# One run for the high halves and one for the low halves in the stream's tile

## The chip, the cores and the metric

The kernel runs on one core of one Trainium2 chip. The metric is the device time of one execution in microseconds; the time before is 2694.59 us, the median of three runs (2694.45 to 2695.38).

## What is computed

One sequence of 256 tokens with 2048 features goes through two blocks. The first is a recurrent branch and a latent attention branch side by side, the second a differential attention layer, a stick-breaking attention layer and a convolutional feed-forward after each. Almost all arithmetic is products of a 256-token activation with a weight matrix of 2048 to 11264 columns:

```python
def second_block(x, positions, ...):
    h = x
    for layer in range(DEPTH_2):
        if layer < N_A_LAYERS:
            xn = _rmsnorm(h, attn_norm_g[layer])
            h = h + _diff_attention(xn, a_w_qkv[layer], ...)
        else:
            if layer == N_A_LAYERS:
                kv = _rmsnorm(h, kv_norm_g) @ b_w_kv
                ...
            xn = _rmsnorm(h, attn_norm_g[layer])
            h = h + _stick_breaking(xn, b_w_q[j], k_shared, v_shared, b_w_o[j])
        h = h + _conv_ffn(_rmsnorm(h, ffn_norm_g[layer]), ffn_w_up[layer], ...)
    return h
```

All tensors are float32, and the kernel has to come near float32 accuracy.

## The kernel before

**Products in halves.** The large products run in the one-pass format fp32r. A weight tile and an activation tile are each split into a high half (the value rounded to fp32r, written by ScalarE) and a low half (the rest, written by VectorE), both float32 words in SBUF. A product is then high x high, high x low and low x high. Line 703 issues two matmuls for each k-tile of 128 features and each block of 128 output rows: a **wide** one, whose moving operand has 512 columns (both halves of one side, against the high half of the other), and a **short** one with 256 columns (the high half of one side against the low half of the other). Their sums stand in the two halves of a PSUM bank and are added on the way out (L1805). In the last k-tile of a product the short one goes first.

**Who moves and who stands.** `unit_product` has two roles. In the usual one the weights (tile `wr`) are loaded into the array and the activation moves; the trace writes this as `acc<-stream,wr` or `acc<-ys,wr`. With `tokens_out` (the value heads of both attention layers) the activation is loaded and the weights move: `acc<-wr,stream`.

**The tiles.** `stream` holds the normalised activation of a layer, 16 k-tiles; in a k-tile its 256 high words are followed by its 256 low words (L363 to L367, `moving_tiles`). `ys` holds the input of an output projection or of a down projection in the same layout. Both begin 80 bytes past a multiple of 256 (`TILES_STEP` 64 and `MOVING_SHIFT` 16). `wr` is a ring of four units of four k-tiles each; its high halves form one run and its low halves another, 8400 bytes further on (`HALF_PAIR`, 2100 words): they begin 16 and 224 bytes past a multiple of 256. A wide matmul of the usual role so reads one run of 512 words, and one of the swapped role reads two runs of 256 words. The k-tiles and the 128-column blocks of all these tiles lie at multiples of 512 bytes from the tile's start, so each operand of a kind has the same place modulo 256 always.

**Order.** Each engine's program is written out by hand and runs in that order; semaphores tie them. SyncE loads `raw` from HBM (L485), ScalarE writes high halves of weights (L1327), VectorE low halves (L1795), TensorE multiplies (L703), VectorE reduces the accumulators (L1805). The activations' halves are written by ScalarE at L1333 (`split`) and by VectorE at L1828 (`lo`): for `stream`, 40 instructions each, two k-tiles at a time. TensorE's loads of the stationary operand (the LDWEIGHTS of each matmul, engine PEld) run beside the matmul ahead of them.

Of the kernel before, what the change touches and what calls it, by code (L numbers as in the profile page):

```python
# [25 lines left out]
P = 128  # L26
# [30 lines left out]
UK = 4  # L57
# [213 lines left out]
WEIGHTS_STEP, TILES_STEP, MOVING_SHIFT = 0, 64, 16  # L271
HALF_PAIR = 2 * UK * 256 + 52
# [32 lines left out]
def program(nc, t, out, consts):  # L305

    ctx = ExitStack()
    with ctx:
# [61 lines left out]
        ys = moving_tiles(nc.alloc_sbuf_tensor_at("ys", [P, GROUP * 2 * TOK + 2 * MOVING_SHIFT // 4], F32R, offset=base), GROUP)  # L370
# [297 lines left out]
        def _(pe):  # L668
# [397 lines left out]
            def woven_product(meanwhile):  # L1066

                T.lo_out.n += KT // 2
                ready, right = T.lo_out.n, lambda k: ys[:, k, :]
# [19 lines left out]
            def residual_product(blocks=KT, stored=False, tiles=2, gates=None, meanwhile=None):  # L1089
# [23 lines left out]
                def two_pairs(first):  # L1113
                    for e in range(2):
# [5 lines left out]
                        pair(lambda k: ys[:, k, :], blocks, before=gated if first and e == 0 else None, after=after)  # L1120
# [45 lines left out]
            def two_heads(first):  # L1166
                for e in range(2):
# [22 lines left out]
                    pair(lambda k: xs[:, k, :], before=None if live else normed, after=in_q)  # L1190
                    pair(lambda k: xs[:, k, :], before=lambda k: diff_sums(0) if k == UK + 1 else None, after=in_k)
                    pair(lambda k: xs[:, k, :], after=in_v, tokens_out=True)
# [18 lines left out]
            def ffn(last):  # L1211
# [8 lines left out]
                for g in range(2):  # L1220
                    if g == 0:
                        pair(lambda k: xs[:, k, :], before=normed_by, after=lambda n: stream_sums() if n == 1 else None)
                        pair(lambda k: xs[:, k, :])
                    with T.turns(pe, GROUP // 2 - (g == 0), **splits(2 * UK), acc_read=2):
                        for e in range(2):
                            pair(lambda k: xs[:, k, :])
# [12 lines left out]
            pair(lambda k: xs[:, k, :], before=normed_by, after=lambda n: stream_sums() if n == 1 else None)  # L1239
            pair(lambda k: xs[:, k, :])  # L1240
            for part in range(2):
                if part == 1:
                    tokens_roots(1 + 3 * A_HEADS + 2)
                with T.turns(pe, B_HEADS // 4 - 1, **splits(8), acc_read=2):
                    for e in range(2):
                        pair(lambda k: xs[:, k, :], tokens_out=part == 1)
            for e in range(2):
                pair(lambda k: xs[:, k, :], tokens_out=True)
# [28 lines left out]
            def two_query_pairs(first):  # L1277

                for e in range(2):
# [11 lines left out]
                    pair(lambda k: xs[:, k, :], before=normed if first and e == 0 else at_tile, after=after)  # L1291
# [19 lines left out]
        def _(act):  # L1311
# [33 lines left out]
            def norm_splits(n):  # L1345

                for _ in range(n):
                    g = norms[0] % (KT // 2)
                    norms[0] += 1
                    split((xs[:, 2 * g:2 * g + 2, 0:TOK], tmp[g % 2][:, :, :]))  # L1350
# [143 lines left out]
            def att_split(it):  # L1494
                act.wait_ge(F.mixed_read.sem, 4 + it)
                f(ys[:, 8 + 2 * it:10 + 2 * it, 0:TOK], tmp[0][:, :, :], ACT.Copy).then_inc(T.hi_out.sem, 1)

            def rnn_split(it):
                split((ys[:, 2 * it:2 * it + 2, 0:TOK], S[1][:, :, :]))
# [51 lines left out]
            def residual_product(units=8, squares=True, stored=False, ahead=0, table=True, woven=False):  # L1551
# [7 lines left out]
                def two_pairs(first, i=None):  # L1559
                    for e in range(2):  # L1560
                        hi(2 if first and woven else units // 2 - (ahead if first and e == 0 else 0))
                        if squares:
# [3 lines left out]
                            split((xs[:, tiles, 0:TOK], tmp[e][:, :, :]))  # L1566
# [44 lines left out]
            def diff_out_split(tiles):  # L1611
                split((ys[:, tiles, 0:TOK], tmp[0][:, :, :]))
# [58 lines left out]
            def ffn(last):  # L1671
                def pair_of_tiles(tile, e, rooted=False):
# [7 lines left out]
                    split((ys[:, tile, 0:TOK], tmp[e][:, 0:1, :]))  # L1680
# [52 lines left out]
            def stick_split(tiles):  # L1733
                split((ys[:, tiles, 0:TOK], tmp[0][:, :, :]))
# [39 lines left out]
        def _(dve):  # L1774
# [50 lines left out]
            def lo(to, src):  # L1825

                dve.wait_ge(*T.hi_out.next())
                tt(to[:, :, TOK:2 * TOK], src, to[:, :, 0:TOK], ALU.subtract).then_inc(*T.lo_out.one())  # L1828

            def norm(value, splits=()):  # L1830

                for g in range(KT // 2 + 1):
# [6 lines left out]
                    if g:  # L1839
                        if g == KT // 2:  # L1840
                            own(T.split_me)
                        lo(xs[:, 2 * g - 2:2 * g, :], tmp[(g - 1) % 2][:, :, :])
# [338 lines left out]
            def att_lo(it):  # L2181
                lo(ys[:, 8 + 2 * it:10 + 2 * it, :], tmp[0][:, :, :])
# [13 lines left out]
            def rnn_lo(i):  # L2196
                own(T.split_me)
                lo(ys[:, 2 * i:2 * i + 2, :], S[1][:, :, :])
# [37 lines left out]
            def residual_product(blocks=KT, gain=None, stored=False, gated=False, first_splits=4, woven=False):  # L2236
# [3 lines left out]
                def two_pairs(first, i=None, final=False):  # L2240
                    for e in range(2):
# [18 lines left out]
                        if gain is not None:  # L2260
# [10 lines left out]
                            lo(xs[:, tiles, :], tmp[e][:, :, :])  # L2271
# [60 lines left out]
            def diff_out_lo(tiles):  # L2332
                own(T.split_me)
                lo(ys[:, tiles, :], tmp[0][:, :, :])
# [52 lines left out]
            def ffn(layer):  # L2387
# [4 lines left out]
                def pair_of_tiles(g, ds, e):  # L2392
# [14 lines left out]
                    lo(ys[:, ds(0), :], tmp[e][:, 0:1, :])  # L2407
# [81 lines left out]
            def stick_lo(tiles):  # L2489
                lo(ys[:, tiles, :], tmp[0][:, :, :])  # L2490
# [73 lines left out]
```

## Time and profile before

| | |
|---|---|
| median of three runs | 2694.59 us |
| the profiled execution | 2694.55 us |
| its span, first to last instruction | 2692.5 us |
| TensorE busy | 2679.0 us, 99% of the span |
| TensorE weight loads | 2345.8 us, 87% |
| VectorE busy | 1978.9 us, 73% |
| ScalarE busy | 1198.1 us, 44% |
| DMA | 64% of the 16 engines' time, 196 GB/s |
| granted clock of TensorE | 1.00 in all slices (2.4 GHz) |

The profile is of one execution. A line of the costliest groups gives the source line, the engine, the operation, the tiles written and read, the size, the count, then busy time and mean duration in ns, then the idle time just before these instructions. The duration of a matmul is from its first column to its last result, and the next one begins long before that: what a matmul costs TensorE is the distance from its start to the next start, and this has to be read from how many of them run in a stretch.

### The profile page before, as it was taken

How to read it: one execution, taken by the hardware profiler on the slowest of the kernel's cores; microseconds unless marked ns; L12 is line 12 of the kernel's file. 1: busy time of each engine (PE TensorE's matmuls, PEld its weight loads, DVE VectorE, ACT ScalarE, POOL GpSimd, SP SyncE). 2: the span in 40 equal slices, each digit the busy share in tenths (PEclk: the TensorE clock that was granted, in tenths of full speed). 3: DMA queues.
4: the chain of work that ended last, by engine and by line, in shares of the span. 5: the costliest groups of instructions: out<-in, count | busy, mean ns of one | idle time of the engine just before them, and what ended most of it. 6: DMA issues, size and time to landing. Idle time of an engine off the chain costs nothing.

```text
span 2692.5 us, 44098 instructions
## 1 busy us (share of the span) xinstructions
PE 2679.0 (99%) x15292; PEld 2345.8 (87%) x15292; DVE 1978.9 (73%) x2594; ACT 1198.1 (44%) x1533; POOL 5.7 (0%) x12
## 2 busy tenths in 40 slices
PE   9999999999999999999999999999999999999999
PEld 7888888888888888888888888888888888888888
DVE  6647577777777788667887676698878876688865
ACT  2004355555554444444444443366444444444443
POOL 0000000000000000000000000000000000000000
PEclk9999999999999999999999999999999999999999
DMA  9986665555556666666666666644566666666664
GB/s 349 358 278 191 204 192 192 163 175 162 161 163 194 190 192 193 197 190 192 193 190 187 201 196 188 190 154 140 186 191 195 193 188 197 188 195 195 191 203 149
DMA packets 705762, 528.14 MB, mean 196 GB/s; under 512 B 32206, under 2 KB 694544, under 8 KB 705424
## 3 DMA queue, kind: packets, MB, share of 16 engines
q1 hardware_dynamic: 701728, 523.60, 63.8%
q10 hardware_dynamic: 3951, 3.44, 0.4%
q8 instruction: 52, 0.85, 0.1%
q14 instruction: 31, 0.25, 0.0%
HBM read 523.80 MB, written 2.10 MB: 195 GB/s over the span
## 4 chain that ended last, share of the span: by engine, by line
PE 96%; DVE 2%; DMA 1%; ACT 0%; issue 0%; SPq 0%; DVEq 0%; ACTq 0%
PE acc L703 81%; PE acc L819 3%; PE acc L1013 2%; PE acc L807 2%; PE turned L819 2%; PE sums L819 2%; PE mixed L934 1%; PE sums L1151 1%; DVE pro_ada L1869 1%; DVE wr L1795 0%; PE scores L1144 0%; PE sums L719 0%; PE mixed L935 0%; DMA pro_xrow<-in_x 0%; PE sums L890 0%; PE scores L920 0%
## 5 line engine op out<-in xcount | busy, mean ns | idle before, releaser
L703 PE MATMUL acc<-stream,wr 128*128 128x512 f32 (+1 forms) x7680 | 1328.5, 333 | 0.3 <-DVE wr L1795 0.3
L703 PEld LDWEIGHTS acc<-stream,wr 128*128 128x128 f32 x7680 | 1159.0, 188 | 156.1 <-issue 3.8
L1795 DVE TENSOR_TENSOR wr<-raw,wr 128x1024 fp32r<-128x1024 f32 x832 | 998.6, 1222 | 317.2 <-ACT wr L1327 307.7
L1327 ACT ACTIVATE wr<-raw 128x1024 fp32r<-128x1024 f32 x832 | 871.2, 1058 | 695.4 <-PE acc L703 682.5
L703 PE MATMUL acc<-ys,wr 128*128 128x512 f32 (+1 forms) x4352 | 747.4, 332 | 0.9 <-DVE wr L1795 0.9
L703 PEld LDWEIGHTS acc<-ys,wr 128*128 128x128 f32 x4352 | 655.7, 188 | 87.3 <-DVE wr L1795 1.5
L703 PE MATMUL acc<-wr,stream 128*128 128x512 f32 (+1 forms) x1024 | 182.7, 338 | 0.0
L703 PEld LDWEIGHTS acc<-wr,stream 128*128 128x128 f32 x1024 | 157.0, 188 | 22.5 <-issue 0.5
L1679 ACT ACTIVATE ffn_cv<-ffn_cv 128x256 f32<-128x256 f32 x88 | 36.9, 419 | 245.5 <-DVE ffn_cv L2401 245.5
L1805 DVE TENSOR_REDUCE ffn_ug<-acc 128x512 f32<-128x1024 f32 x88 | 107.8, 1225 | 35.2 <-PE acc L703 35.2
L1828 DVE TENSOR_TENSOR ys<-tmp,ys 128x256 f32 (+3 forms) x108 | 51.3, 475 | 76.0 <-ACT ys L1333 73.4
L1869 DVE SCALAR_TENSOR_TENSOR pro_ada<-aring,small,pro_ada 128x512 f32<-128x512 f32 (+1 forms) x103 | 85.7, 833 | 22.9 <-DMA aring<-in_w_ada 17.0
L1805 DVE TENSOR_REDUCE S<-acc 128x512 f32<-128x1024 f32 x72 | 87.9, 1221 | 19.7 <-PE acc L703 19.7
L1333 ACT ACTIVATE ys<-tmp 128x256 f32 (+3 forms) x104 | 46.8, 450 | 106.4 <-DVE tmp L2405 102.0
L1809 DVE TENSOR_TENSOR ffn_ug<-ffn_ug,rx 128x512 f32<-128x512 f32 x88 | 60.9, 692 | 3.0
L807 PE MATMUL acc<-xm,w 128*128 128x256 f32 x256 | 58.4, 381 | 0.7 <-DVE xm L1889 0.4
L1013 PE MATMUL acc<-xm,w 128*128 128x256 f32 x256 | 57.3, 379 | 0.0
L807 PEld LDWEIGHTS acc<-xm,w 128*128 128x128 f32 x256 | 48.2, 190 | 8.9 <-issue 1.9
L1013 PEld LDWEIGHTS acc<-xm,w 128*128 128x128 f32 x256 | 47.7, 190 | 6.0
L2399 DVE SCALAR_TENSOR_TENSOR ffn_cv<-ffn_ug,vcol,ffn_cv 128x256 f32<-128x256 f32 x88 | 42.7, 485 | 13.2 <-DVE ffn_cv L2396 13.0
L2401 DVE SCALAR_TENSOR_TENSOR ffn_cv<-ffn_ug,vcol,ffn_cv 128x256 f32<-128x256 f32 x88 | 42.7, 485 | 13.0 <-DVE ffn_cv L2399 12.8
L2396 DVE TENSOR_SCALAR ffn_cv<-ffn_ug,vcol 128x256 f32<-128x256 f32 x88 | 36.4, 413 | 16.5 <-DVE ffn_ug L1809 16.4
(324 smaller groups left out, 1482.9 us busy)
## 6 DMA issues: line engine op xcount, KB each, us to landing
raw<-in_ffn_w_up SPq DMA_DIRECT2D x704, 256.0 KB
raw<-in_ffn_w_down SPq DMA_DIRECT2D x160, 512.0 KB
raw<-in_a_w_qkv SPq DMA_DIRECT2D x96, 512.0 KB
raw<-in_b_w_kv SPq DMA_DIRECT2D x64, 512.0 KB
aring<-in_w_ada SPq DMA_DIRECT2D x96, 256.0 KB, 6.6
w<-in_w_in SPq DMA_DIRECT2D x48, 512.0 KB
raw<-in_w_ada SPq DMA_DIRECT2D x32, 512.0 KB, 4.9
raw<-in_w_out SPq DMA_DIRECT2D x32, 512.0 KB
```

The costliest lines, as they stand in the source:

```text
L703: mm = pe.matmul(*ops, start=first and ops is wide, stop=last and ops is wide)
L807: pe.matmul(bank(c // 2)[:, (c % 2) * TOK:(c % 2 + 1) * TOK], w[:, c * P:(c + 1) * P], xm[:, k, :], start=False, stop=k == KT - 1 and c % ...
L819: mm = pe.matmul(out(j), *here, start=k == 0, stop=k == UK - 1)
L1013: mm = pe.matmul(bank(b + j)[:, 0:TOK], w[:, k, j * P:(j + 1) * P], xm[:, u * UK + k, :], start=u == 0 and k == 0, stop=u == 3 and k == UK ...
L1327: f(half_of(0, s), raw[:, s, :], ACT.Copy)\
L1333: f(to[0], to[1], ACT.Copy).then_inc(T.hi_out.sem, 1)
L1795: tt(half_of(1, s), raw[:, s, :], half_of(0, s), ALU.subtract).then_inc(T.unit_split[s].sem, 1)
L1805: dve.tensor_reduce(out_tiles, a[:, 0:tiles, :].rearrange("p t (b c) -> p t c b", b=2), axis=AX_X, op=ALU.add)\
L1809: tt(out_tiles, out_tiles, both(rx), ALU.mult).then_inc(*T.acc_read.one())
L1828: tt(to[:, :, TOK:2 * TOK], src, to[:, :, 0:TOK], ALU.subtract).then_inc(*T.lo_out.one())
L1869: stt(here, aring[:, n % ADA_RING, 0:2 * kn * P], small[:, 8 + r:9 + r], here, ALU.mult, ALU.add)\
L2399: step(stt(cv[e][:, :], UG[e][:, 1, 1:1 + TOK], taps[1], cv[e][:, :], ALU.mult, ALU.add))
```

## The change

The tile `stream` gets another layout: the high halves of all 16 k-tiles stand in one run of 16384 bytes, the low halves in a second run that begins 128 bytes after the end of the first. High halves begin at the same 80 bytes modulo 256 as before; low halves began at 80 too and now begin at 208. The tile is 256 bytes longer, so what is allocated behind it keeps its place modulo 256. `ys` and `wr` stay as they are; `ys` is only indexed with one dimension more.

```diff
@@ -269,6 +269,7 @@
 WEIGHTS_STEP, TILES_STEP, MOVING_SHIFT = 0, 64, 16
+LOWS_SHIFT = 128
 HALF_PAIR = 2 * UK * 256 + 52
@@ -356,18 +357,18 @@
-        stream = sb("stream", [KT * 2 * TOK + 2 * MOVING_SHIFT // 4], F32R)
-        xs_at = nc.sbuf_base - KT * 2 * TOK * 4 - 2 * MOVING_SHIFT
-
-        def moving_tiles(tensor, tiles):
-
-            return tensor[:, MOVING_SHIFT // 4:MOVING_SHIFT // 4 + tiles * 2 * TOK].rearrange("p (k n) -> p k n", k=tiles)
-
-        xs = moving_tiles(stream, KT)
+        run = KT * TOK + LOWS_SHIFT // 4
+        stream = sb("stream", [2 * run + 2 * MOVING_SHIFT // 4], F32R)
+        xs_at = nc.sbuf_base - 2 * run * 4 - 2 * MOVING_SHIFT
+
+        xs = stream[:, MOVING_SHIFT // 4:MOVING_SHIFT // 4 + 2 * run].rearrange("p (h r) -> p h r", h=2)[:, :, 0:KT * TOK]\
+            .rearrange("p h (k n) -> p k h n", k=KT)
@@ -694,11 +695,11 @@
                         if tokens_out:
-                            wide = (a[:, j, :], x[:, cols], both_halves)
-                            short = (a[:, j, 0:256], x[:, 256 + j * P:256 + j * P + P], high)
+                            wide = (a[:, j, :], x[:, 0, cols], both_halves)
+                            short = (a[:, j, 0:256], x[:, 1, cols], high)
                         else:
                             wide = (a[:, j, :], high[:, cols], x)
-                            short = (a[:, j, 0:256], low[:, cols], x[:, 0:TOK])
+                            short = (a[:, j, 0:256], low[:, cols], x[:, 0, :])
@@ -1825,7 +1826,7 @@
-                tt(to[:, :, TOK:2 * TOK], src, to[:, :, 0:TOK], ALU.subtract).then_inc(*T.lo_out.one())
+                tt(to[:, :, 1, :], src, to[:, :, 0, :], ALU.subtract).then_inc(*T.lo_out.one())
```

The rest of the diff is the same change of index at each use of `xs` and `ys`. No instruction is moved, and each engine's program has the same operations in the same order and of the same sizes. Two things differ in form: the halves that ScalarE and VectorE write to `stream` are one run of 512 words (two k-tiles) instead of two runs of 256, and VectorE issues 8 register instructions fewer for their addresses.

## Rows read from the trace of the kernel before

**Rows 1.** The page: engines, share of the span, and TensorE's granted clock
```profile
PE 2679.0 (99%) x15292; PEld 2345.8 (87%) x15292; DVE 1978.9 (73%) x2594; ACT 1198.1 (44%) x1533; POOL 5.7 (0%) x12
...
PEclk9999999999999999999999999999999999999999
```

**Rows 2.** The page: the chain that ended last, by engine and line
```profile
PE 96%; DVE 2%; DMA 1%; ACT 0%; issue 0%; SPq 0%; DVEq 0%; ACTq 0%
PE acc L703 81%; PE acc L819 3%; PE acc L1013 2%; PE acc L807 2%; PE turned L819 2%; PE sums L819 2%; PE mixed L934 1%; PE sums L1151 1%; DVE pro_ada L1869 1%; DVE wr L1795 0%; PE scores L1144 0%; PE sums L719 0%; PE mixed L935 0%; DMA pro_xrow<-in_x 0%; PE sums L890 0%; PE scores L920 0%
```

**Rows 3.** TensorE's groups by shape over the whole span (count | busy us, mean ns)
```profile
L703 PE MATMUL acc<-stream,wr 128*128 128x512 f32 x3840 | 1314.9, 391 | 0.3 <-DVE wr L1795 0.3
L703 PE MATMUL acc<-stream,wr 128*128 128x256 f32 x3840 | 1037.9, 275 | 0.0
L703 PE MATMUL acc<-ys,wr 128*128 128x512 f32 x2176 | 741.6, 389 | 0.9 <-DVE wr L1795 0.9
L703 PE MATMUL acc<-ys,wr 128*128 128x256 f32 x2176 | 590.0, 275 | 0.0
L703 PE MATMUL acc<-wr,stream 128*128 128x512 f32 x512 | 180.6, 396 | 0.0
L703 PE MATMUL acc<-wr,stream 128*128 128x256 f32 x512 | 140.8, 280 | 0.0
```

**Rows 4.** Matmuls running in stretches of 85 us: usual role (stream), swapped role, usual role (ys)
```profile
1240.00:1325.00 85.00, 85.00 (x501) 1.00 0.68 194
1668.00:1753.00 85.00, 85.00 (x488) 1.00 0.62 186
1110.00:1195.00 85.00, 85.00 (x501) 1.00 0.63 195
```

**Rows 5.** Groups by shape in 1240 to 1325 us, usual role
```profile
L703 PE MATMUL acc<-stream,wr 128*128 128x512 f32 x251 | 85.0, 388 | 0.0
...
L703 PE MATMUL acc<-stream,wr 128*128 128x256 f32 x250 | 67.7, 275 | 0.0
```

**Rows 6.** Groups by shape in 1668 to 1753 us, swapped role
```profile
L703 PE MATMUL acc<-wr,stream 128*128 128x512 f32 x244 | 84.8, 394 | 0.0
...
L703 PE MATMUL acc<-wr,stream 128*128 128x256 f32 x244 | 67.2, 280 | 0.0
```

**Rows 7.** Plain float32 matmuls of 256 columns in 110 to 125 us
```profile
110.00:125.00 15.00, 15.00 (x71) 1.00 1.06 403
```

**Rows 8.** ScalarE's and VectorE's writes to stream and ys, by shape
```profile
L1333 ACT ACTIVATE stream<-tmp 128x512 f32 x24 | 15.2, 634 | 3.7 <-DVE tmp L2263 0.9
L1828 DVE TENSOR_TENSOR stream<-tmp,stream 128x512 f32 x24 | 16.6, 693 | 7.4 <-ACT stream L1333 7.4
L1809 DVE TENSOR_TENSOR S<-S,rx 128x512 f32<-128x512 f32 x16 | 11.1, 692 | 0.5
L1600 ACT ACTIVATE sq<-S 128x512 f32<-128x512 f32 x16 | 10.1, 632 | 16.1 <-DVE S L1809 16.1
```

**Rows 9.** All waits of TensorE: who it waited for, us, times, longest
```profile
PE turned L724 <- DMA cst<-in_constants: 4.9, 1, 4.9
PE turned L1110 <- DVE ffn_fin L2258: 2.0, 1, 2.0
PE acc L703 <- DVE wr L1795: 1.2, 3, 0.5
```

More of the change, by code:

```diff
@@ L1119, in after @@
                                 meanwhile(n)
-                        pair(lambda k: ys[:, k, :], blocks, before=gated if first and e == 0 else None, after=after)
+                        pair(lambda k: ys[:, k, :, :], blocks, before=gated if first and e == 0 else None, after=after)
                 per = dict(acc_read=2, **splits(2 * -(-blocks // UK)))
@@ L1188, in in_v @@
                             diff_out_sums()
-                    pair(lambda k: xs[:, k, :], before=None if live else normed, after=in_q)
-                    pair(lambda k: xs[:, k, :], before=lambda k: diff_sums(0) if k == UK + 1 else None, after=in_k)
-                    pair(lambda k: xs[:, k, :], after=in_v, tokens_out=True)
+                    pair(lambda k: xs[:, k, :, :], before=None if live else normed, after=in_q)
+                    pair(lambda k: xs[:, k, :, :], before=lambda k: diff_sums(0) if k == UK + 1 else None, after=in_k)
+                    pair(lambda k: xs[:, k, :, :], after=in_v, tokens_out=True)
             two_heads(True)
@@ L1221, in ffn @@
                     if g == 0:
-                        pair(lambda k: xs[:, k, :], before=normed_by, after=lambda n: stream_sums() if n == 1 else None)
-                        pair(lambda k: xs[:, k, :])
+                        pair(lambda k: xs[:, k, :, :], before=normed_by, after=lambda n: stream_sums() if n == 1 else None)
+                        pair(lambda k: xs[:, k, :, :])
                     with T.turns(pe, GROUP // 2 - (g == 0), **splits(2 * UK), acc_read=2):
                         for e in range(2):
-                            pair(lambda k: xs[:, k, :])
+                            pair(lambda k: xs[:, k, :, :])
                     residual_product(GROUP, stored=g == 1 and last, tiles=1)
@@ L1237, in normed_by @@
                     pe.wait_ge(T.lo_out.sem, ready + k // 2 + 1)
-            pair(lambda k: xs[:, k, :], before=normed_by, after=lambda n: stream_sums() if n == 1 else None)
-            pair(lambda k: xs[:, k, :])
+            pair(lambda k: xs[:, k, :, :], before=normed_by, after=lambda n: stream_sums() if n == 1 else None)
+            pair(lambda k: xs[:, k, :, :])
             for part in range(2):
@@ L1245, in _ @@
                     for e in range(2):
-                        pair(lambda k: xs[:, k, :], tokens_out=part == 1)
+                        pair(lambda k: xs[:, k, :, :], tokens_out=part == 1)
             for e in range(2):
-                pair(lambda k: xs[:, k, :], tokens_out=True)
+                pair(lambda k: xs[:, k, :, :], tokens_out=True)
             def stick_scores():
@@ L1290, in at_tile @@
                             stick_sums(0)
-                    pair(lambda k: xs[:, k, :], before=normed if first and e == 0 else at_tile, after=after)
+                    pair(lambda k: xs[:, k, :, :], before=normed if first and e == 0 else at_tile, after=after)
             two_query_pairs(True)
@@ L1611, in diff_out_split @@
             def diff_out_split(tiles):
-                split((ys[:, tiles, 0:TOK], tmp[0][:, :, :]))
+                split((ys[:, tiles, 0, :], tmp[0][:, :, :]))
             def two_heads(first, i=None):
@@ L1733, in stick_split @@
             def stick_split(tiles):
-                split((ys[:, tiles, 0:TOK], tmp[0][:, :, :]))
+                split((ys[:, tiles, 0, :], tmp[0][:, :, :]))
             def two_query_pairs(first, i=None):
@@ L2181, in att_lo @@
             def att_lo(it):
-                lo(ys[:, 8 + 2 * it:10 + 2 * it, :], tmp[0][:, :, :])
+                lo(ys[:, 8 + 2 * it:10 + 2 * it, :, :], tmp[0][:, :, :])
             def rnn_gate(i):
@@ L2197, in rnn_lo @@
                 own(T.split_me)
-                lo(ys[:, 2 * i:2 * i + 2, :], S[1][:, :, :])
+                lo(ys[:, 2 * i:2 * i + 2, :, :], S[1][:, :, :])
             F.scores_ready.n, F.scores_read.n = 8, 8
@@ L2333, in diff_out_lo @@
                 own(T.split_me)
-                lo(ys[:, tiles, :], tmp[0][:, :, :])
+                lo(ys[:, tiles, :, :], tmp[0][:, :, :])
             def two_heads(first, i=None):
@@ L2406, in pair_of_tiles @@
                     own(T.split_me)
-                    lo(ys[:, ds(0), :], tmp[e][:, 0:1, :])
+                    lo(ys[:, ds(0), :, :], tmp[e][:, 0:1, :])
                     split_units(3)
@@ L2489, in stick_lo @@
             def stick_lo(tiles):
-                lo(ys[:, tiles, :], tmp[0][:, :, :])
+                lo(ys[:, tiles, :, :], tmp[0][:, :, :])
             def two_query_pairs(first, i=None):
```

19 lines of the change are left out of this document (10 added, 9 removed).

## The prediction

> **What bounds the kernel now.** I read the engines' line first: TensorE is busy 2679.0 us of 2692.5, at a granted clock of full speed in every slice [rows 1]. That line alone would not do, since matmuls are recorded with their latency and overlap, so I looked at the chain that ended last, which is TensorE for 96% and line 703 for 81% [rows 2], and at TensorE's waits, the longest three of which add up to 8.1 us in the whole program [rows 9]. So nothing is gained by making another engine faster, and each nanosecond on a matmul of line 703 is a nanosecond of the kernel. What one costs is read from a stretch in which nothing else runs. In 85 us of the usual role 501 matmuls are running [rows 4], that is 250.5 pairs of a wide and a short one, or 339.3 ns a pair; `ys` gives the same count. In 85 us of the swapped role there are 488, or 244 pairs of 348.4 ns. (Each count takes in the one or two that run across the edge, in all three stretches alike; so the difference, 9.1 ns, is better than the level.) The whole program has 3840 pairs in the usual role on `stream`, 2176 on `ys` and 512 in the swapped role [rows 3].
>
> **What the change touches.** Four things, and no instruction count or order on TensorE, ScalarE, SyncE or GpSimd.
>
> First, the moving operand of 3840 wide matmuls is two runs of 256 words, the second 128 bytes further on modulo 256, instead of one run of 512. Usual pairs with two runs do not occur in the trace of before, so the price is bounded by the nearest rows. Wide matmuls with two runs exist in the swapped role, there with 208 bytes between the places: their mean is 394 ns against 388 for those with one run, 6 ns more [rows 5, 6]. But the short matmuls beside them, which read a single run in both roles, are slower by 280 - 275 = 5 ns as well [rows 5, 6]. So what the swapped role pays is paid by both kinds, and the part that only the jump between two runs can have caused is 6 - 5 = 1 ns at most, within the rounding of the rows. The whole-span rows say the same: 396 - 391 = 5 and 280 - 275 = 5, so 0 [rows 3]. The 5 ns that both pay I put down to how the loaded and the moving operand lie to each other, since this is what differs for both: in the usual role the moving words begin at 80 and the loaded ones at 16 or 224 modulo 256, in the swapped one the moving ones at 16 and the loaded ones at 80. The value I take for the jump is 0 ns. The ends are: up, 3840 x 9.1 ns = +35 us, if all of the swapped role's surplus comes from jumps; down, what the low half of a wide matmul could at best give back. For that the nearest row is the plain float32 matmuls, which pass 256 columns twice: 71 are running in 15 us, 211 ns each, or near 216 with the two at the edges left out, so 108 ns for a pass of 256 columns [rows 7]. A third of an fp32r pair is 339.3 / 3 = 113.1 ns. The low half of a wide one could so fall by 113 - 108 = 5 ns, 3840 x 5 = -19 us, and no run of 256 fp32r columns in the usual role is that fast in these rows.
>
> Second, in the swapped role the low half of the activation is the loaded operand of the 512 short matmuls, and its place goes from 80 to 208. It is loaded while the wide one before it runs, whose first run begins at 16. The distance of moving to loaded was 16 - 80 = 192 modulo 256; it becomes 16 - 208 = 64. In the usual role the high weights are loaded under a short matmul at 80 - 16 = 64, and those pay nothing. If 64 is good here too, the surplus of the wide matmul, about half of the 9.1 ns of the pair, goes: 512 x 4.5 = -2.3 us. The high half stays at 80, and the short ones keep their 5 ns. The ends are 0 and 512 x 9.1 = -4.7 us, or the same the other way, +2.3 us, if the new place is the worse.
>
> The Trainium skill (SBUF — State Buffer, section "A bandwidth-pool intuition that's wrong") gives TensorE a read port for the moving operand and a second, independent one for LDWEIGHTS. By that rule no place of one can matter for the other, this term would be 0, and the total below would be higher by its 2.3 us. The rows speak against it: the same short matmul with 256 columns takes 280 ns in one role and 275 in the other [rows 5, 6].
>
> Third, ScalarE's and VectorE's 40 writes each to `stream` become one run of 512 words. With two runs they take 634 and 693 ns; the same operations on one run of 512 take 632 and 692 [rows 8]. So 80 instructions gain 1 to 2 ns each, 0.1 us, and most lie beside matmuls. TensorE is not among those that wait for them in its three longest waits [rows 9]. 0 us.
>
> Fourth, 8 register instructions fewer on VectorE, which stands idle 27% of the span [rows 1]: 0 us. The waits do not change, since the same semaphores count the same instructions.
>
> The sum: 0 - 2.3 + 0 + 0 = -2.3 us. The profiled execution took 2694.55 us, 2.05 more than its span and 0.04 less than the median of the runs; so 2694.55 - 2.3 = 2692.3 us, and the same against the median. What a measurement here can tell from no change is about 0.2%, or 5.4 us: this is the same time.
>
> **The rivals.** *The jumps cost.* The swapped role is then slow because the place modulo 256 changes inside each wide matmul and again at the next short one, and reading has to fall into step again; the short ones' 5 ns are the step back. In the usual role everything moving began at 80 modulo 256 and nothing ever changed its place; after the change it goes 80, 208, 80 in every pair. For it: the two roles differ in this more than in anything else, and it explains both 5 ns at once. Against it: within the swapped role the step forward (208 bytes) and the step back (48) are unlike, and cost the same 5 ns. Its price is 3840 x 9.1 = +35 us, so 2692.3 + 35 = 2727 us; at half the price, with only the wide ones paying, +17 and 2710 us. It decides the sign from 1.4 ns a pair (5.4 us / 3840) on, with the 2.3 us of the swapped role kept.
>
> *The usual role gets faster.* An fp32r pair takes 339.3 ns where three passes at the pace of the float32 rows are 3 x 108 = 324 [rows 4, 7]. If what slows them is a clash between reads of the moving and of the loaded operand, a low half at another place than the high half can miss the clash. With the low half of the wide one relieved of 5 ns this gives 2692.3 - 19 = 2673 us. Against it: the load of 128 columns runs beside the first part of a wide matmul, and the low half is its second part; and stream and ys, in different places of SBUF and with different work beside them, both stand at 501 in 85 us [rows 4], which looks like a pace of the format rather than a clash. The Trainium skill (TensorE: Matmul & The Clock Gate, section "Back-to-back issue gap") has N/2.4 + 2.5 ns for one matmul. By it a wide and a short one would take 215.8 + 109.2 = 325 ns, an estimate from that page, and the kernel stands 14 ns a pair above it; nothing in it says that a layout could get there.
>
> *It does nothing at all,* also not in the swapped role: the ports are independent and both surpluses come from the format of the operands. Then 2694.6 us.
>
> **How the numbers follow.** The forecast (jump free, the swapped role gains some) has 0.44, with its own range of 2688 to 2698 from the ends of the second term and 1 ns on the first. Nothing at all has 0.05. The jumps cost their full price: 0.14. They cost between 1 and 5 ns a pair (+4 to +19 us): 0.13, nearly all of it over 0.2%. The usual role gets faster: 0.24, mostly between -6 and -26 us. Adding up by sign: faster by over 0.2% (under 2689.2 us) 0.24 and 0.02 of the forecast's lower edge, 0.26; slower by over 0.2% (over 2700.0) 0.14 + 0.12 = 0.26 and 0.01, so 0.27; the rest, 0.47, is the same. The likeliest is the forecast, 2692.3. The range goes from 2668 (a gain of 5 ns a wide matmul and a little on the short ones) to 2730 (the full price of the jumps and 3 us): outside are some 0.07 of larger gains and 0.05 of larger losses.
>
> **What would show it.** The count of matmuls in 85 us of a feed-forward stretch on `stream` is the test: 501 again for the forecast, 488 for jumps at full price, 505 or more where the usual role gets faster (85 us / 334 ns is 254 pairs, 508). The stretches on `ys` must stay at 501; should they move too, it is not the layout of `stream`. In the swapped role the count should go from 488 to 494 or so (85 us / 343.9 ns), with the wide ones' mean down from 394 towards 389 and the short ones at 280. ScalarE's L1333 and VectorE's L1828 should stand at 632 and 692 ns. The prediction is wrong from its first term if the wide matmuls' mean on `stream` leaves 388 ns by more than 1.

## The result and the profile after

The changed kernel takes 2725.77 us (median of five runs, 2725.38 to 2726.08), the kernel before 2694.79 us in the same comparison (2694.45 to 2695.38): a ratio of 1.0115, 95% interval 1.0104 to 1.0126. It is 31.0 us slower. The forecast of "the same" was wrong; the time is close to the one of the first rival, 2727 us, and inside the stated range (2668 to 2730) only because that rival's full price set its upper end.

The page of the changed kernel, engines and clock, to be laid beside [rows 1]:

```profile
PE 2711.6 (100%) x15292; PEld 2363.6 (87%) x15292; DVE 1981.3 (73%) x2594; ACT 1198.5 (44%) x1533; POOL 5.7 (0%) x12
...
PEclk9999999999999999999999999999999999999999
```

TensorE is busy 32.6 us longer with the same 15292 matmuls at the same granted clock, and the other engines do what they did. TensorE's groups by shape over the whole span, to be laid beside [rows 3]:

```profile
L704 PE MATMUL acc<-stream,wr 128*128 128x512 f32 x3840 | 1343.2, 395 | 0.1
L704 PE MATMUL acc<-stream,wr 128*128 128x256 f32 x3840 | 1054.8, 280 | 0.0
L704 PE MATMUL acc<-ys,wr 128*128 128x512 f32 x2176 | 741.9, 389 | 0.9 <-DVE wr L1796 0.9
L704 PE MATMUL acc<-ys,wr 128*128 128x256 f32 x2176 | 590.2, 275 | 0.0
L704 PE MATMUL acc<-wr,stream 128*128 128x512 f32 x512 | 182.2, 398 | 0.0
L704 PE MATMUL acc<-wr,stream 128*128 128x256 f32 x512 | 141.2, 281 | 0.0
```

Nearly all of the loss is on the stream in the usual role: the recorded durations of the wide matmuls go from 391 to 395 ns, and those of the short ones, whose moving words, loaded words and places have not changed at all, from 275 to 280. The `ys` groups stand where they stood. The matmuls running in 85 us show the price; the second stretch lies a little later than in [rows 4], since the swapped role now comes later (columns: stretch, its length, TensorE busy and matmuls running, clock, DMA share, GB/s):

```profile
1240.00:1325.00 85.00, 85.00 (x489) 1.00 0.64 182
1690.00:1775.00 85.00, 85.00 (x484) 1.00 0.61 185
1110.00:1195.00 85.00, 85.00 (x502) 1.00 0.62 194
```

On the stream 489 for 501: 2 x 85 us / 489 = 347.7 ns a pair, 8.3 ns more, x 3840 pairs = +32 us. In the swapped role 484 for 488: 351.2 ns a pair, 2.8 ns more, x 512 = +1.4 us, where a gain of 2.3 had been forecast. `ys` stands at 502 for 501. These sum to 33 us. TensorE is busy 32.6 us longer and idle 1.0 us less (12.5 us for 13.5), so the span grew by 2724.1 - 2692.5 = 31.6 us. Counts of whole matmuls are no better than 0.7 ns a pair. ScalarE's and VectorE's writes to the stream are unchanged, where the third term had them 1 to 2 ns shorter, without any consequence for the time [rows 8]:

```profile
L1829 DVE TENSOR_TENSOR stream<-tmp,stream 128x512 f32 x24 | 16.6, 693 | 5.1 <-ACT stream L1334 4.9
...
L1334 ACT ACTIVATE stream<-tmp 128x512 f32 x24 | 15.2, 634 | 3.1
```

So all of the time is in how close matmuls of the stream follow each other. In what follows a tile's price is its pair time less that of the kernel before, counted in two stretches that lie within the same stage in every kernel: 1245 to 1330 us for the stream and 1120 to 1205 us for `ys`. The kernel before has there

```profile
1245.00:1330.00 85.00, 85.00 (x501) 1.00 0.67 191
1120.00:1205.00 85.00, 85.00 (x502) 1.00 0.63 195
```

so 339.3 and 338.6 ns a pair, and the changed one

```profile
1245.00:1330.00 85.00, 85.00 (x489) 1.00 0.65 187
1120.00:1205.00 85.00, 85.00 (x502) 1.00 0.63 195
```

One matmul more or less is 0.7 ns a pair. "Place" is where a tile's words begin, modulo 256 bytes. The places of before: moving 80, high weights 16, low weights 224.

A count gives the price of a pair, and a recorded duration does not give that of one matmul. For this the trace's start times serve: the mean distance from the start of a matmul to the start of the next one, over all neighbouring pairs of the stream in the usual role (3671 or 3672 distances of either kind; those over 300 ns, where TensorE paused, are left out). The level comes out 1 ns higher than by the counts.

| kernel | wide to next, ns | short to next, ns | pair, ns |
|---|---|---|---|
| before | 227.0 | 113.8 | 340.8 |
| changed (low run at 208) | 231.8 | 117.1 | 349.0 |
| only the short one at 208 | 231.7 | 115.3 | 347.1 |
| only the wide one at 208 | 232.1 | 117.9 | 350.0 |
| all at 208 | 232.9 | 119.7 | 352.5 |
| changed, low run at 64 | 228.7 | 116.1 | 344.9 |
| changed, low run at 16 | 226.9 | 114.5 | 341.4 |
| before, one-word loads | 229.4 | 117.7 | 347.1 |
| changed, one-word loads | 232.7 | 114.2 | 346.9 |

So the untouched short matmuls of the changed kernel do cost TensorE more, 3.3 ns each, beside 4.8 ns for the wide ones. The kernels below the first two are those of the experiments.

**The other engines do not make the price.** ScalarE, VectorE and DMA read and write SBUF all the while, so their accesses might be what the low run at 208 collides with. The two traces settle it. The distance from the start of a wide matmul to the start of the next wide one, on the stream, sorted by what else ran in it (number of pairs in brackets; those over 420 ns left out):

| during the pair | before, ns | changed, ns |
|---|---|---|
| VectorE runs nothing | 340.0 (265) | 348.2 (315) |
| VectorE runs throughout | 341.0 (2121) | 349.0 (1868) |
| ScalarE runs nothing | 340.0 (1258) | 348.0 (1365) |
| ScalarE runs throughout | 341.1 (1254) | 348.9 (1141) |
| no DMA packet on its way | 341.1 (489) | 348.9 (584) |

The change costs 8 ns in every row, whether the other engine works or not.

### The profile page after: what moved, and what is told of

The parts are those of the page before. It is cut to its first block, busy times and chain, and to the rows that moved or that the text cites. A ratio compares the mean times of both kernels' runs of the same rounds, so it can differ in the third digit from the quotient of the medians.

```text
span 2724.1 us, 44074 instructions
## 1 busy us (share of the span) xinstructions
PE 2711.6 (100%) x15292; PEld 2363.6 (87%) x15292; DVE 1981.3 (73%) x2594; ACT 1198.5 (44%) x1533; POOL 5.7 (0%) x12
## 4 chain that ended last, share of the span: by engine, by line
PE 98%; DVE 2%; ACT 0%; issue 0%; DMA 0%; DVEq 0%; SPq 0%; ACTq 0%
PE acc L704 82%; PE acc L820 3%; PE acc L1014 2%; PE acc L808 2%; PE turned L820 2%; PE sums L820 2%; PE mixed L935 1%; PE sums L1152 1%; DVE pro_ada L1870 0%; PE scores L1145 0%; PE sums L720 0%; PE mixed L936 0%; PE sums L891 0%; PE scores L921 0%; DVE wr L1796 0%; PE acc L729 0%
## 5 line engine op out<-in xcount | busy, mean ns | idle before, releaser
L704 PE MATMUL acc<-stream,wr 128*128 128x512 f32 (+1 forms) x7680 | 1359.0, 338 | 0.1
L704 PEld LDWEIGHTS acc<-stream,wr 128*128 128x128 f32 x7680 | 1175.3, 188 | 169.8 <-issue 3.8
```

## The experiments

The recorded expectations speak of three theories. Theory A: a change of the moving operand's place costs. Theory B: the place of the moving words relative to the loaded ones costs. Theory C: two runs far apart cost, wherever they lie. Where no number of executions is given, a time is of one execution; 13 executions of the kernel before lay between 2694.15 and 2695.18 us.

### Are two runs, or their places, the cause?

**Two runs at one place.** The changed kernel with

```diff
-LOWS_SHIFT = 128
+LOWS_SHIFT = 0
```

> The changed kernel with the shift between the runs at 0 instead of 128: two runs, 16384 bytes apart, both beginning at 80 modulo 256. Theory A (what costs is that the moving operand's place modulo 256 changes, inside a wide matmul and at the next short one): no change of place, so 2694.8 us, the time of before, and 501 matmuls in 85 us. Theory B (the low run's place clashes with the weights being loaded beside it): also 2694.8 us. Theory C (two runs far apart are slow as such, wherever they lie): 2725 us, 489 in 85 us.

Measured 2694.45 us (median of 10) against 2694.38 (13), ratio 0.9999, interval 0.9990 to 1.0009. The stretch of the stream, in this kernel:

```profile
1245.00:1330.00 85.00, 85.00 (x501) 1.00 0.67 191
```

Two runs as such, 16 KB apart, cost nothing. Theory C is out, and the whole 31 us hang on the 128 bytes.

**The low run at 144.** The same line with 64 (place 80 + 64 = 144).

> The changed kernel with a shift of 64 bytes instead of 128, low run at 144 modulo 256. Theory A: slower than before, by half of 31 us or more, 2710 to 2726 us, if the cost grows with the distance modulo 256, and by the same 31 us if any change of place costs. Theory B: anything from 2695 to 2730 us, since another place may or may not clash. Theory C: 2725 us.

2728.55 us, 34 us slower; 490 on the stream. A smaller step than 128 costs no less, so the price does not grow with the step. Either any step costs, or certain places do.

**No step at all, but another place.** The kernel before with

```diff
-        begin_at("stream_gap", TILES_STEP)
+        begin_at("stream_gap", TILES_STEP + 128)
```

> The kernel of before, one run of high and low in each k-tile, with the whole stream tile 128 bytes further on modulo 256: all moving words of the stream begin at 208. No change of place inside or between matmuls of the stream, but all of them at the place of the changed kernel's low run. Theory A: 2694.8 us within 3 us (only the loaded operand of the swapped role moves). Theory B: as slow as the changed kernel or slower, 2725 us and more. Theory C: 2694.8 us.

2738.20 us, 43.8 us slower than its 2694.38. All moving words of the stream begin at 208, none changes place, and it is slower than the changed kernel. Its stretch on the stream and its groups:

```profile
1245.00:1330.00 85.00, 85.00 (x485) 1.00 0.63 182
```
```profile
L703 PE MATMUL acc<-stream,wr 128*128 128x512 f32 x3840 | 1358.0, 396 | 0.0
L703 PE MATMUL acc<-stream,wr 128*128 128x256 f32 x3840 | 1061.2, 281 | 0.0
```

Theory A, the rival that had come nearest to the time, falls as the sole cause: a step is not needed for the price.

**Only the short ones, only the wide ones.** The kernel before, with the short matmul of the stream reading from 208, and then (with the tile at 208) the wide one reading from 208 and the short one from 80:

```diff
-                            short = (a[:, j, 0:256], low[:, cols], x[:, 0:TOK])
+                            short = (a[:, j, 0:256], low[:, cols], x[:, 32:32 + TOK] if x.tensor.name == 'stream' else x[:, 0:TOK])
```

> The kernel of before with one edit: in the usual role on the stream the short matmul reads 256 words that begin 128 bytes further on (at 208 modulo 256) than the high half it should read; so low weights x high activation is left out of the product and 224 high and 32 low words are multiplied instead. Wide matmuls have one run at 80. The place changes between matmuls only, twice a pair. Theory A: 31 us slower, 2725 us, as the changed kernel, since the same two changes of place occur in a pair. Theory B: the wide ones untouched, the short ones perhaps slower, 2695 to 2715 us. Theory C: 2694.8 us.

> The complement of the displaced short matmul: on the stream the wide one reads one run at 208 modulo 256, the short one 256 words at 80 (the stream's tile is at 208 and the short one reads 128 bytes further on, so part of low weights x high activation is left out). Theory A: the same two changes of place in a pair as in the changed kernel, 2725 us. Theory B: wide ones at distance 208 - 224 = 240, short ones at 64: the wide one's share of what the stream at 208 cost, between 2705 and 2738 us; by differences of the runs so far 43.8 - 22.7 = 21 us, so 2716 us.

2717.14 us and 2727.83 us: 22.8 and 33.1 us slower, 5.9 and 8.6 ns a pair. With only the short one displaced the groups are:

```profile
L703 PE MATMUL acc<-stream,wr 128*128 128x512 f32 x3840 | 1337.6, 396 | 0.2 <-DVE wr L1795 0.2
L703 PE MATMUL acc<-stream,wr 128*128 128x256 f32 x3840 | 1046.1, 278 | 0.0
```

It is the wide ones, which were not touched, that pay more, and the displaced short ones less: start to start the wide ones take 4.7 ns more than before and the short ones 1.5 (recorded durations 391 to 396 and 275 to 278). And the two prices do not add: 22.8 + 33.1 = 55.9 us where both together, the stream at 208, cost 43.8. The price of a pair is a matter of the whole pattern of places, not a sum over its matmuls. Neither theory had that.

### Does the distance to the loaded weights count?

**Moving and loaded words together.** The kernel before with the stream and all weights 128 bytes further on:

```diff
-WEIGHTS_STEP, TILES_STEP, MOVING_SHIFT = 0, 64, 16
+WEIGHTS_STEP, TILES_STEP, MOVING_SHIFT = 128, 64, 16
...
-        begin_at("stream_gap", TILES_STEP)
+        begin_at("stream_gap", TILES_STEP + 128)
```

> The kernel of before with stream and weights both 128 bytes further on (stream 208, weights 144 and 96), ys left at 80. Nothing is left out of the computation. Theory A: 2694.8 us, no place changes within or between matmuls. Theory B: stream pairs 340 ns since all distances are kept, ys pairs about 351 ns since theirs are those of the stream in the kernel with the stream at 208 (43.8 us / 3840 = 11.4 ns a pair); 2176 x 11.4 = +25 us, so near 2719 us. A theory by which the place alone decides (208 is bad in itself): stream slow, ys fast, 2738 us.

2718.99 us, where theory B had 2719. Stream, then `ys`:

```profile
1245.00:1330.00 85.00, 85.00 (x501) 1.00 0.68 194
1120.00:1205.00 85.00, 85.00 (x485) 1.00 0.59 186
```

The stream at 208, which cost 11 ns a pair above, is back at 501 once the weights have moved along. `ys`, which has not moved, now has the 485 that the stream had there. So it is not the place 80 or 208 by itself that is good or bad; it is how moving and loaded words lie to each other.

**Distances kept, places changing.** The kernel with the displaced short matmul, and the high weights at 144:

```diff
-HALF_PAIR = 2 * UK * 256 + 52
-WEIGHTS_SHIFT = 4
-SLOT_PAIR = -(-2 * HALF_PAIR // 64) * 64
+HALF_PAIR = 2 * UK * 256 + 20
+WEIGHTS_SHIFT = 36
+SLOT_PAIR = 4224
```

> The kernel with the displaced short matmul (it reads 256 words from 208 modulo 256 on in place of the high half at 80; low weights x high activation is so left out on the stream), and now the weights' high halves at 144 instead of 16; their low halves stay at 224. On the stream each matmul keeps the distance of before between moving words and the weights loaded beside them (short 208 - 144 = 64, wide 80 - 224 = 112 modulo 256), though the place changes by 128 at every matmul. On ys nothing is displaced, so the short one there is at 80 - 144 = 192. Theory A (changes of place cost): stream pairs about 346 to 349 ns, ys pairs 340. Theory B (the distance moving - loaded decides): stream pairs 340 ns, ys pairs 346 ns, as the displaced short one cost (22.7 us / 3840 = 5.9 ns a pair).

2734.29 us, stream 489 (8.3 ns) and `ys` 497 (3.4 ns):

```profile
1245.00:1330.00 85.00, 85.00 (x489) 1.00 0.64 184
1120.00:1205.00 85.00, 85.00 (x497) 1.00 0.62 193
```

Theory B had the stream at 501 and `ys` slow. The distance of each matmul to the load that runs beside it, taken by itself, does not give the price.

**Loads that stay on one word.** Each matmul of the usual role loads one word 128 times, in the old layout and in the new one:

```diff
-                            wide = (a[:, j, :], high[:, cols], x)
-                            short = (a[:, j, 0:256], low[:, cols], x[:, 0:TOK])
+                            wide = (a[:, j, :], high[:, j * P:j * P + 1].to_broadcast([P, P]), x)
+                            short = (a[:, j, 0:256], low[:, j * P:j * P + 1].to_broadcast([P, P]), x[:, 0:TOK])
```

> The kernel of before; in the usual role each matmul loads one word of its weights 128 times (step 0) instead of 128 words, so the products are those of one weight column, 127 of 128 columns left out; moving reads, counts and order as before. If the loads' reads walk into the moving reads, a load that stays on one word clashes otherwise: the pairs leave 340 ns, downwards at most to about 324. If the pace of 340 ns is the format's own, it stays at 340.

> The changed kernel with the same one-word loads. Clash of loads and moving reads (theory B): the 8 ns a pair between the layouts vanish or change much, so this and the one before it take the same time within 5 us. Change of place of the moving operand alone (theory A), no load needed: the 31 us between them stay.

2731.05 us with the old layout and 2730.61 us with the new one. The stream's stretch in the old layout, then in the new one:

```profile
1245.00:1330.00 85.00, 85.00 (x491) 1.00 0.63 180
1245.00:1330.00 85.00, 85.00 (x493) 1.00 0.64 182
```

The 31 us between the layouts are gone, though the moving operands are read exactly as before in each. Pairs of the stream take 346.2 ns (491) in the old layout and 344.8 (493) in the new one. So what the loads read matters for the pace. This pair of runs alone doesn't show how: a load that stays on one word is no relief but costs 36.3 us / 6016 pairs = 6.0 ns itself in the old layout, and start to start it is shared out differently in the two (2.4 ns on the wide and 3.9 on the short ones in the old layout, 5.7 and 0.4 over the kernel before in the new one). That both sums come out alike may be chance. The firmer evidence that moving and loaded words make the price together is the run that moved them together. What the pace would be without loads is not shown.

### How do the places compare?

**All moving words at another place.** The kernel before with other steps at `slab_gap` (for `ys`) and `stream_gap`, and for 64 and 96 with the first word of each tile moved by 16 bytes. Each run gives two places, one for each tile:

```diff
-        begin_at("slab_gap", TILES_STEP)
+        begin_at("slab_gap", 96)
...
-        begin_at("stream_gap", TILES_STEP)
+        begin_at("stream_gap", 128)
```

> The kernel of before with ys at 112 and the stream at 144 modulo 256, each one run, nothing left out: two more points of the price against the distance (short 96 and 128, wide 144 and 176 modulo 256). Theory A: 2694.8 us. Theory B: each tile's pairs get a price of their own between 340 and 351 ns, and the swapped role (moving 16, loaded 144, distance 128) gets another one than its 349 ns of before.

> The kernel of before with ys at 16 and the stream at 48 modulo 256, nothing left out. Two more points of the price against the place of the moving operand where no place ever changes. So far, in surplus over the 340 ns of before per pair: 80 gives 0, 112 gives 9, 144 gives 12, 208 gives 11.7. Theory B (distance moving - loaded decides): each has a price of its own between 0 and 13 ns; 48 is next to 80 and may be cheap. A theory that the price rises smoothly with the distance from 80 gives 48 the 9 ns of 112.

> As before this one, with ys at 176 and the stream at 240 modulo 256. Theory B: between 0 and 13 ns a pair each. If 80 is the one place in this layout that costs nothing, both are above 5 ns and the kernel is above 2720 us.

> The kernel of before with ys at 64 and the stream at 96 modulo 256, each in one run, nothing left out: 16 bytes off the good place on either side. If the good place is narrow, both cost 3 to 9 ns a pair (ys at 112 and 48 cost 9 and 11); if it is a plateau, one of them stays at 340 ns; if it is the edge of one, one of them is under 340 ns and the kernel could be made faster.

They took 2759.76, 2745.42, 2766.29 and 2750.14 us. The price of each place, where nothing changes place within a pair (2 x 85 us / count, less the same tile's pair time before); 208 is from the run above:

| place of all moving words | 16 | 48 | 64 | 80 | 96 | 112 | 144 | 176 | 208 | 240 |
|---|---|---|---|---|---|---|---|---|---|---|
| tile | ys | stream | ys | both | stream | ys | stream | ys | stream | stream |
| matmuls in 85 us | 491 | 485 | 490 | 501, 502 | 485 | 489 | 483 | 483 | 485 | 484 |
| price, ns a pair | 7.6 | 11.2 | 8.3 | 0 | 11.2 | 9.0 | 12.7 | 13.3 | 11.2 | 11.9 |

With the weights at 16 and 224 no place tried but 80 is free for all moving words, and 16 bytes to either side already cost 8 (on `ys`) and 11 ns (on the stream). With both tiles elsewhere the kernel is 51 to 72 us slower than the 2694.7 us beside it, and at no place is it faster. In the slowest of these kernels (`ys` 176, stream 240):

```profile
1245.00:1330.00 85.00, 85.00 (x484) 1.00 0.64 185
1120.00:1205.00 85.00, 85.00 (x483) 1.00 0.60 186
```

One thing got faster. The swapped role reads weights from 16 and 224 and loads words of the stream, so it changes too when the stream moves. With the stream at 48 its groups are

```profile
L703 PE MATMUL acc<-wr,stream 128*128 128x512 f32 x512 | 178.3, 394 | 0.0
L703 PE MATMUL acc<-wr,stream 128*128 128x256 f32 x512 | 139.6, 278 | 0.0
```

where they were 396 and 280 [rows 3]; start to start its pair takes 344.7 ns, 4.6 less than the 349.3 of before. That is about 512 x 4.6 = 2.4 us, while the usual role loses far more at that place.

**The low run alone at other places.** The changed kernel with 240 and with 192 for its 128:

> The changed kernel with a shift of 240 instead of 128: the low run at 64 modulo 256, 16 bytes off the place of the high run. A price that grows with the distance: 1 ns a pair, 2699 us. A pattern that any other place breaks: 5 ns a pair or more, 2714 us and more.

> The changed kernel with a shift of 192: the low run at 16, 64 bytes off on the other side than the shift of 64, which cost 34 us. Price by the size of the distance: the same 34 us, 2729 us. Price by the distance to the weights loaded (16 - 224 = 48): anything from 2695 to 2740 us.

2710.84 us with the low run at 64, 16 bytes off (496 on the stream); 2696.98 us with it at 16, 64 bytes off. The stream's stretch in the second of these, and its groups:

```profile
1245.00:1330.00 85.00, 85.00 (x501) 1.00 0.67 191
```
```profile
L704 PE MATMUL acc<-stream,wr 128*128 128x512 f32 x3840 | 1316.9, 391 | 0.3 <-DVE wr L1796 0.3
L704 PE MATMUL acc<-stream,wr 128*128 128x256 f32 x3840 | 1042.3, 276 | 0.0
```

The place steps by 64 bytes back inside each wide matmul and forth again after it, 7680 times, and the stream is at 501; start to start its pair takes 341.4 ns for 340.8. Two steps of place a pair and the new place of the low run together so cost 0.6 ns, or 2.3 us: a step has no price that must be paid. It is also a second pattern that is all but free, beside the one with all moving words at 80. The kernel with the low run at 16 (a step of 64 bytes) is 2.3 us slower than the one before, at 64 (a step of 16) 16.1 us, at 144 (64) 34 and at 208 (128) 31 us. The price does not follow the size of the step.

### Which load is it?

**The low weights 128 bytes on.** The changed kernel with low weights at 96, as far from the low run (208 - 96 = 112) as they had been from the high one:

```diff
-HALF_PAIR = 2 * UK * 256 + 52
+HALF_PAIR = 2 * UK * 256 + 20
...
-SLOT_PAIR = -(-2 * HALF_PAIR // 64) * 64
+SLOT_PAIR = 4224
```

> The changed kernel with the weights' low halves at 96 instead of 224 modulo 256, nothing left out. Theory B1 (the load of low weights clashes with the wide matmul's low half, by their distance alone): on the stream that distance is 208 - 96 = 112 again, as in the kernel before, so stream pairs come back to 340 ns; on ys (80 - 96 = 240) pairs cost as much as the changed kernel's, 348 ns. Theory B2 (the load meets the high half in its first part and everything after depends on the whole pattern of places): both stream and ys are slow, 345 to 353 ns a pair, and the kernel is over 2735 us.

2737.31 us; stream 492 (6.2 ns), `ys` 488 (9.7 ns). The stream does not come back: theory B1, by which the distance to the low weights alone decides, falls. B2 holds, which only says that the whole pattern counts.

**One kind of load on one word.** The changed kernel, with the one-word edit on the low weights alone and on the high weights alone:

> The changed kernel with one-word loads of the low weights only (the load that runs beside the wide matmul; 127 of 128 low columns are left out), high weights loaded in full. If the clash is of this load with the wide matmul, the difference between stream and ys in pair time, 8 ns in the changed kernel, goes to under 2 ns. If it is the other load's, it stays at 6 to 10 ns.

> The changed kernel with one-word loads of the high weights only (the load that runs beside the short matmul), low weights loaded in full. The mirror of the one before: the difference between stream and ys stays at 6 to 10 ns if the load beside the wide matmul is the one that clashes, and goes to under 2 ns if it is this one. If both leave 3 to 6 ns, both loads take part.

2741.27 us and 2730.27 us. Stream and `ys` stand at 487 and 494 with low weights on one word, 5 ns a pair apart, and at 492 and 493 with high weights on one word, 0.7 ns apart. The 0.7 ns are under the mark of 2 ns, which spoke for the load of the high weights (the one beside the short matmul). The 5 ns lie between the marks (under 2, or 6 to 10), and start to start they are 3.5; so it isn't shown that the load of the low weights has no part. And in both runs `ys` itself costs 5.5 and 6.2 ns, so the good pattern is broken for the control too. The pair is inconclusive.

## Why the prediction was wrong

**What bounds the kernel** held: the runs' times follow TensorE's pace on line 703, and the counts in 85 us, named beforehand as the test, show which tile pays in each.

**The first term failed.** Its value was 0 ns for the second run; measured is 8.3 ns a pair, 32 us. (The sign of failure that was named beforehand came: the wide matmuls' mean in 1240 to 1325 us is 393 ns, 5 over 388.) The step of the working that failed is the subtraction 6 - 5 = 1 ns: I took the wide matmuls' surplus in the swapped role, took away what the short ones pay as well, and called the rest the price of the new place. That assumes that a matmul pays for its own operands. It does not: in the changed kernel the short matmuls have the operands of before and cost 3.3 ns more from start to start, and with only the short one displaced the wide ones cost 4.7 more. So "both kinds pay it" was no reason to take the 5 ns off the price of the change. What the swapped role pays depends on places too: its pair went from 349.3 to 344.7 ns with the stream at 48. The upper end, 9.1 ns a pair, was near the measured 8.3, and lay in the text as the price of a rival with a chance of 0.14 whose reason was wrong: that the two agree is luck.

**The reason given for the 5 ns was nearly right** and was then used for the wrong matmuls. "How the loaded and the moving operand lie to each other" is what the moved-together run confirms. But having said so I should have asked what the low run at 208 is to the weights at 16 and 224: 192 and 240. The first of these distances the kernel before had in the swapped role alone, the slow one; the second it had nowhere. I left it out because the load seemed to run beside the first part of a wide matmul only. The trace of before spoke against that:

```profile
L703 PEld LDWEIGHTS acc<-stream,wr 128*128 128x128 f32 x7680 | 1159.0, 188 | 156.1 <-issue 3.8 <-DVE wr L1795 0.7
```

A load is recorded for 188 ns and starts 2 to 3 ns (median) after the start of the matmul beside it. A wide one takes 227 ns to the next start, so half of it is over after 113. And the load that starts beside a short matmul, which takes 114 ns, is recorded until some 75 ns into the next wide one. When within the 188 ns a load reads is not shown, but the changed kernel shows that the second part of a wide matmul counts.

**The second term failed in sign.** The swapped role was to gain 2.3 us and lost 1.4. The loss of 1.4 is two of the count's steps; start to start it is 3.5 ns a pair, 1.8 us. "If 64 is good here too" took one distance out of a pattern of several. The run with kept distances refutes such a rule: each matmul kept its distance to the load beside it, and the stream still cost 8.3 ns.

**The rivals.** "The jumps cost" named nearly the right time for the wrong reason: it gives its price to two changes of place in a pair, and the low run at 16 has just as many and costs 2.3 us, the stream at 208 has none and costs 44. "The usual role gets faster" did not come about at any of ten places for all moving words, nor at any of four other places for the low run; the 324 ns that three float32 passes would take [rows 7] were reached nowhere, and whether 340 ns is the format's own pace is not shown, since the loads could not be taken away. "It does nothing" falls. The Trainium skill (SBUF — State Buffer, section "A bandwidth-pool intuition that's wrong") gives TensorE a second, independent read port for LDWEIGHTS. If that meant, as the prediction took it, that the place of one operand can't matter for the other, the traces do not agree: the stream at 208 stands at 485 with the weights at 16 and 224 and at 501 with the weights at 144 and 96.

**Third and fourth** were put at 0 us and held: the page shows the other engines' busy times within 2.4 us of before, and the writes to the stream at their old durations.

**What stays open** is the mechanism: how the reads of a load and of a moving run get in each other's way. Shown is that the price depends on how moving and loaded words lie to each other, that it belongs to a whole pattern and not to one matmul's distance, and that work of the other engines doesn't make it. That what the loads read changes the pace is shown too, by the 6 ns of the one-word runs; that the 31 us need both reads is what these and the moved-together run fit, without proving it. Which load meets which half is not settled. Nor is the period: places are counted modulo 256 bytes here, but no run moved a tile by 256 bytes alone.

No kernel that ran is faster than the one before; the one with two runs at one place equals it.

## What to carry to other kernels

In this kernel, where TensorE is busy all the time with one-pass fp32r matmuls, the start of the moving tile relative to the weight tile is worth as much as 13 ns in 340. It could not be worked out from a few distances. Where it may matter, sweep it in steps of 16 bytes or less, one tile at a time, with a second tile left alone as the control. And when a price is read off a neighbouring case, don't subtract what its neighbours pay too: ask first whether they pay for the same thing. A surplus that two kinds of matmul share may be exactly the cost that the change brings. Last, count matmuls in a stretch of fixed length, or take distances from start to start; the recorded duration of a single one does not say what it costs.

## What the runs showed of the hardware

- A pair of a 512-column and a 256-column fp32r matmul took 339 to 341 ns in the good patterns (moving words at 80, or the low run at 16, with weights at 16 and 224; all moved by 128 bytes) and up to 352 ns in others, at a granted clock of 1.00 (2.4 GHz) throughout.
- An operand's place shows in its neighbours: with only the short matmuls of the stream displaced by 128 bytes, the untouched wide ones took 4.7 ns more from start to start (231.7 for 227.0) and the displaced ones 1.5 more (115.3 for 113.8).
- The 8 ns of the changed layout are the same in pairs during which VectorE, ScalarE or DMA did nothing (348.2, 348.0 and 348.9 ns, for 340.0, 340.0 and 341.1 before).
- In the swapped role a pair took 349.3 ns with the loaded stream at 80 and 344.7 with it at 48.
- Ten places 16 to 32 bytes apart were tried for a whole moving tile, and one was free. 16 bytes off it cost 8.3 ns (64, `ys`) and 11.2 ns (96, stream) a pair.
- Loading one word 128 times instead of 128 words cost 6 ns a pair in the layout of before, and with it the two layouts took the same time (2731.05 and 2730.61 us).
- A matmul's moving operand in two runs 16 KB apart cost the same as in one run, where both began at 80 modulo 256 (2694.45 against 2694.38 us).
